# A two-block transformer kernel on one core: retention recast for whole-array matmuls, stick attention's first head readied early, and three smaller edits

## The reference

```python
# experts: out = hb @ w_down, summed with gates; then x = rms_norm(x + y, g_final),
# and the second block begins with h = rms_norm(x, pre_norm_w)
# retention, 4 heads, key width 64, value width 128, chunks of C = 128 tokens
q = rotary(q); k = rotary(k) * (dk ** -0.5)
scores = einsum('bhnid,bhnjd->bhnij', qc, kc) * decay
o_intra = einsum('bhnij,bhnje->bhnie', scores, vc)
chunk_kv = einsum('bhnjd,hj,bhnje->nbhde', kc, k_decay, vc)
state = state * g_chunk + kv                       # over the 8 chunks
o_inter = einsum('bhnid,hi,nbhde->bhnie', qc, q_decay, r_prev)
# stick-breaking attention, 8 heads of width 64
z = einsum('bthd,bshd->bhts', q, k) * scale        # then sigmoids, a reversed
                                                   # running product, and w @ v
# hgrn2, 4 heads: products of q and k with exp of differences of b = cumsum(log_f)
```

## Time and profile before

| what | us |
|---|---|
| median of 3 runs (lowest, highest) | 2588.99 (2585.32, 2596.64) |
| the profiled execution, its own time | 2613.81 |
| its span, first to last instruction | 2612.0 |
| busy: TensorE, VectorE, ScalarE, GpSimd | 2218.1, 1290.0, 1029.8, 584.1 |
| experts' last output copy to first product of `pe` | 1235.96 to 1290.39 |
| retention, first to last TensorE work | 1628.97 to 1699.43 |
| stick attention, first TensorE work | 1715.47 |
| HGRN2, first TensorE work | 2354.51 |

### The profile page before, as it was taken

How to read it: one execution, slowest core, us unless ns; L and a number is a source line. 1 busy time by engine, 2 the same in 40 slices (tenths; PEclk the granted TensorE clock), 3 DMA queues, 4 the chain that set the end, 5 groups by cost and what they waited for, 6 DMA issues and landing times. The chain is left out here.

```text
span 2612.0 us, 34392 instructions
## 1 busy us (share of the span) xinstructions
PE 2218.1 (85%) x12244; PEld 1825.9 (70%) x12244; DVE 1290.0 (49%) x2211; ACT 1029.8 (39%) x1828; POOL 584.1 (22%) x672
## 2 busy tenths in 40 slices
PE   7996997999797599999289997968859799956768
PEld 5885887999685466675278885758748687845657
DVE  3333665555543666665451210357755343417843
ACT  3333654555431255554231210046543233327632
POOL 1003101522010122231110001446522000027822
PEclk9997998999898699999699998579989899987879
DMA  4787776321344399995652312243163424141152
GB/s 152 215 239 198 221 219 165 98 64 40 118 146 171 126 359 370 355 342 209 217 206 97 113 49 77 61 87 73 37 219 108 153 95 148 69 135 47 42 184 90
DMA packets 216721, 399.15 MB, mean 153 GB/s; under 512 B 90513, under 2 KB 111377, under 8 KB 203905
## 3 DMA queue, kind: packets, MB, share of 16 engines
q1 hardware_dynamic: 177008, 314.52, 38.0%
q10 hardware_dynamic: 28384, 61.62, 6.2%
q0 software_dynamic: 11184, 21.13, 2.2%
HBM read 300.16 MB, written 114.85 MB: 159 GB/s over the span
## 5 line engine op out<-in xcount | busy, mean ns | idle before, releaser
L78 PE MATMUL pe_acc<-pe_w,hT 128*128 128x512 f32 x960 | 222.3, 393 | 0.0
L78 PEld LDWEIGHTS pe_acc<-pe_w,hT 128*128 128x128 f32 x960 | 181.7, 190 | 37.8
L78 PE MATMUL ex_gu<-hT,ex_xT 128*128 128x512 f32 x792 | 194.2, 401 | 0.8 <-DVE hT L2349 0.8
L2349 DVE TENSOR_TENSOR hT<-ex_raw,hT 128x2048 fp32r<-128x2048 f32 x66 | 150.9, 2288 | 87.1 <-ACT hT L2320 87.1
L78 PE MATMUL pg_acc<-hT,pg_w 128*128 128x512 f32 x768 | 180.0, 396 | 8.9 <-DVE pg_w L257 8.9
L78 PEld LDWEIGHTS pg_acc<-hT,pg_w 128*128 128x128 f32 x768 | 145.5, 190 | 42.4 <-DVE pg_w L257 9.3
L78 PEld LDWEIGHTS ex_gu<-hT,ex_xT 128*128 128x128 f32 x792 | 147.4, 189 | 34.5 <-DVE hT L2349 1.2
L2320 ACT ACTIVATE hT<-ex_raw 128x2048 fp32r<-128x2048 f32 x66 | 126.2, 1913 | 41.4 <-PEq L47 23.9
L296 DVE COPY pe_o<-pe_acc 128x512 f32<-128x512 f32 x28 | 19.3, 690 | 206.7 <-PE pe_acc L78 206.7
L1725 PE MATMUL ab_op<-ab_v,ab_pT 128*128 128x64 f32 x1024 | 121.3, 272 | 0.0
L2278 PE MATMUL ex_dn<-ex_wd,ex_hT 128*128 128x512 f32 x264 | 118.7, 592 | 0.8 <-ACT ex_hT L2314 0.8
(11 more groups left out here) (473 smaller groups left out, 4990.9 us busy)
## 6 DMA issues: line engine op xcount, KB each, us to landing
ex_raw<-in_w_gate SPq DMA_DIRECT2D x33, 1024.0 KB, 7.2
ex_raw<-in_w_up SPq DMA_DIRECT2D x33, 1024.0 KB, 11.1
ex_wd<-in_w_down SPq DMA_DIRECT2D x33, 1024.0 KB, 14.2
pe_raw<-in_even_w_in SPq DMA_DIRECT2D x6, 2048.0 KB, 9.1
pg_raw<-in_odd_w_in SPq DMA_DIRECT2D x5, 2048.0 KB, 9.4
scr_q<-pa_o SPq DMA_DIRECT2D x32, 256.0 KB, 3.8
scr_k<-pa_o SPq DMA_DIRECT2D x32, 256.0 KB, 3.8
hT<-scr_k SPq DMA_DIRECT2D x16, 512.0 KB, 6.8
```

The source lines that it names most:

```text
L78: mm = pe.matmul(out, a(p, k), b(q, k), start=(k == 0 and i == 0), stop=(k == n - 1 and i == 2))
L2349: dve.tensor_tensor(split(s, LO)[:, :, g, :], raw[:, s % NW, g, :].rearrange("p (k n) -> p k n", k=8), split(s, HI)[:, :, g, :].bitcast(F3 ...
```

## The change

Five edits.

1. **Retention.** Keys are copied into `kz`, one full 128-row block per head with zeros in the other head's 64 rows, and `state` gets a block per head with such zeros, so that scores and q x state contract over 128 rows. The copies from PSUM move from VectorE to ScalarE (four per tile). GpSimd keeps half of the rotation, VectorE takes the other. The state update is four instructions over 64 partitions in place of two over 128. SP loads the first tile ahead of the constants.
2. **Stick attention's first head** is loaded, rounded (ScalarE, at tiles 3 and 4) and its remainders formed (GpSimd, after its rotations) within the retention, into three blocks of hT. The stick stage starts without these steps.
3. **Norms ahead of a projection.** With expert rows, ScalarE does `z` (`act_z`). The first tile's turn comes right behind the weight split on ScalarE and VectorE, and TensorE starts the first product with the first tile alone, doing the second tile's turn after 6 of its 8 blocks. The gain row `prow` is loaded after the first tile's rows.
4. **The loop `further`** has 7 passes with two bodies under one test in place of 14.
5. **HGRN2.** One subtraction per level over all 512, and the sign goes into two Exps of 256. In the first unit VectorE multiplies the keys (`keys_first`), GpSimd the queries.

```diff
@@ project, TensorE @@
+                def first_steps(k):
+                    pe.wait_ge(lo_ok, k + 1)
+                    if r and k == nk - 2:
+                        r.pe_turn(pe, 1)
...
-                            for t in range(j + 1 if j else 0, min(j + 2, NT)):
+                            for t in range(j + 1 if j else 0, min(j + 2, NT) if j else 1):
                                 r.pe_turn(pe, t)
@@ project, ScalarE @@
-                        at_step(s, (r.act_turn, lx + 2, act), (r.act_x, lx, act), (r.act_y, 0, act))
+                        if s > lx + 2:
+                            at_step(s, (r.act_turn, lx + 2, act))
+                        elif lx and s == 2:
+                            r.act_turn(act, 0)
+                        if lx and s > lx + 1:
+                            at_step(s, (r.act_z, lx + 1, act))
+                        at_step(s, (r.act_x, lx, act), (r.act_y, 0, act))
                         if s == 1:
+                            if lx:
+                                r.act_z(act, 0)
                             gains(act)
                             split_hi(act, 0)
+                            if not lx:
+                                r.act_turn(act, 0)
@@ project, VectorE @@
                             split_lo(dve, 0)
-                        at_step(s, (r.dve_turn, lx + 2, dve), (r.dve_x, lx, dve), (r.dve_y, 0, dve))
+                            r.dve_turn(dve, 0)
+                        if s > lx + 2:
+                            at_step(s, (r.dve_turn, lx + 2, dve))
+                        at_step(s, (r.dve_x, lx, dve), (r.dve_y, 0, dve))
@@ Rows @@
+    def act_z(self, act, t):
+        act.wait_ge(self.rs_ok, t + 1)
+        self.x_done(act, t)
+        if t >= 2:
+            act.wait_ge(self.turned, t - 1)
+        for n, (c0, w) in enumerate(self.groups):
+            act.activation(self.z[:, t % 2, c0:c0 + w], self.xs[:, u, c0:c0 + w], ACT.Copy,
+                           scale=self.rs[:, u, n:n + 1]).then_inc(self.z_ok, 1)
@@ further @@
-            with eng.Fori(1, NOV) as j:
-                with eng.If(n > j):
-                    body(j)
+            with eng.Fori(0, (NOV - 1) // 2) as r:
+                with eng.If(n > r * 2 + 1):
+                    for i in range(2):
+                        body(r * 2 + (i + 1))
@@ retention @@
+            def rotate(eng, t, products, step, op, c0, a, b):
+                eng.wait_ge(x_in[t % 4], 16 * (t // 4 + 1))
...
+                eng.tensor_tensor(a[:, u, :, :], first[0], first[1], ALU.mult).then_inc(products, 1)
+                eng.tensor_tensor(b[:, u, :, :], second[0], second[1], ALU.mult).then_inc(products, 1)
+                eng.wait_ge(products, 2 * (t + 1))
+                eng.tensor_tensor(rot[:, t % 4, :, c0:c0 + 32], a[:, u, :, :], b[:, u, :, :], op).then_inc(step, 1)
...
-                            mm = pe.matmul(o, qkT[p0:p0 + 64, u, 4 + j, :], state[p0:p0 + 64, u, j, :], start=False, stop=True)
+                            mm = pe.matmul(o, qkT[:, u, 2 + j, :], state[:, u, h, :], start=False, stop=True)
...
-                            mm = pe.matmul(sps[h % 2][:, j * P:(j + 1) * P], qkT[p0:p0 + 64, u, 2 + j, :], qkT[p0:p0 + 64, u, j, :],
-                                           start=True, stop=True)
+                            mm = pe.matmul(sps[h % 2][:, j * P:(j + 1) * P], kz[:, u, h, :], qkT[:, u, j, :], start=True, stop=True)
...
+                def turn_back(s):
...
+                    act.activation(qkT[:, u, 0:2, :].rearrange("p j n -> p (j n)"), tp[0][:, 0:2 * P], ACT.Copy).then_inc(T_ok, 1)
+                    for b in range(2):
+                        r = slice(64 * b, 64 * b + 64)
+                        act.activation(kz[r, u, :, :].rearrange("p (j b) n -> p j b n", b=2)[:, :, b, :],
+                                       tp[0][r, 2 * P:4 * P].rearrange("p (j n) -> p j n", j=2), ACT.Copy).then_inc(T_ok, 1)
+                    act.activation(qkT[:, u, 2:4, :].rearrange("p j n -> p (j n)"), tp[1][:, 0:2 * P], ACT.Copy).then_inc(T_ok, 1)
@@ stick_breaking, SP @@
-                load_raw(0, 0)
                 sp.dma_start(masks[:, :, :], C["strict"]).then_inc(consts_in, 16)
+                sp.sem_inc(raw_in[0], 64)
+                sp.sem_inc(hi_ok, 8)
+                sp.sem_inc(lo_ok, 8)
@@ hgrn2 @@
-                        act.activation(ex[:, g % 2, :], df[:, g % 2, :], ACT.Exp).then_inc(ex_ok, 1)
+                        for half, sign in enumerate((-1.0, 1.0)):
+                            act.activation(ev[:, :, half, :], dv[:, :, half, :], ACT.Exp, scale=sign).then_inc(ex_ok, 1)
...
-                        dve.tensor_tensor(dv[:, :, 0, :], mid, bv[:, :, 0, :], ALU.subtract).then_inc(df_ok, 1)
-                        dve.tensor_tensor(dv[:, :, 1, :], bv[:, :, 1, :], mid, ALU.subtract).then_inc(df_ok, 1)
+                        dve.tensor_tensor(whole(df[:, g % 2, :], m), whole(b[:, :], m), mid, ALU.subtract).then_inc(df_ok, 1)
+                        if n == 0 and l:
+                            keys_first(l - 1)
```

176 lines of the change are left out of this document (112 added, 64 removed).

## The result

The changed kernel takes 2572.15 us (median of 4 executions, 2562.74 to 2575.03) beside 2590.68 us for the kernel before (4 executions, 2585.32 to 2596.64): a ratio of 0.992, 95% interval 0.9891 to 0.9949. It is faster by 18.5 us, where 47 were forecast; 2572.15 lies above the range of 2532 to 2564. Two later comparisons of the same two kernels gave 0.988 (0.9852 to 0.9907) and 0.9917 (0.9887 to 0.9948). All 19 executions of the changed kernel have a median of 2571.8 us, the 92 of the kernel before in the later comparisons 2591.7: 20 us.

The account below looks back on a forecast made before the run. TensorE was taken as the bound, slowed in the retention by half clock and drains. Terms -29 - 8 - 7 + 0.5 + 0 - 3.5 = -47 us took the median from 2588.99 to 2542, range 2532 to 2564.

Parts of the forecast that it names:

- Gain 29: Whole retention with its earlier start: ends about 1670 in place of 1699.43 us; gain 12 if never at full clock.
- Which clock: Retention: without drains the array works 95% of a step, not 70%, so full clock comes after two steps.
- Retention, one step: Padding removes tiling-mode drains: step 7.6 us for 9.17 at half clock; at full clock TensorE 4.0, step taken as 4.8.
- Retention, whole stage: Retention from first transposes to last output: 45 us, with first scores after 5, one step at 7.6, six at 4.8.
- Retention, start: First tile's rows load first and VectorE shares the rotation: TensorE starts at 1624.5 for 1628.97, gain 4.5 us.
- Stick attention's start: Seam after the retention: first head's loads, roundings and remainders leave the path, masks come first; gain 8 us.
- The loop: Behind the experts: 14 passes at 1.0 us each become seven, 7 us less; nothing if cost follows code jumped over.
- Start of `pe`: Projection behind the experts: first rows 1.7 us sooner, later xs 2.2 us later; net +0.5 us, ends -2 and +3.
- First projection: TensorE begins 1.6 us sooner and waits as long later: 0, ends -1 and +1 us.
- HGRN2: First unit 2.7 us less, later levels 2 less at best, ScalarE 1 more: -3.5 us, ends -6 and +2.
- The rivals: Other outcomes: clock stays half 2559 us (0.25), seams only 2566.5 (0.09), edits not as said 2583 (0.05), slower 2602 (0.01).
- Only the seams gain: Rival, chance 0.09: retention step stays at 9.17 us, set by something else; 22.5 us remain, giving 2566.5.

Follow-up runs that it names:

- before_again: The kernel before, unchanged, run and profiled once more: median 2594.3 us over 12 executions, ratio 1.0003 to the kernel before.
- ret_only: The kernel before with the changed retention alone, stick attention's lead work done in it for nothing: 2584.4 us, ratio 0.9971 to the kernel before.
- ret_old: The changed kernel with the old retention, stick attention's first head still readied inside it: 2580.3 us, ratio 0.9925 to the kernel before.
- after_again: The changed kernel, unchanged, run and profiled once more: 2566.6 us, ratio 0.988 to the kernel before.
- norms_old: The changed kernel with the old order of projections and norms (gain row first, z on VectorE, second transpose group before first product): 2570.1 us, ratio 0.9902 to before.
- after_third: The changed kernel, unchanged, run and profiled a third time: 2572.3 us, ratio 0.9917 to the kernel before.
- before_warm: The kernel before with 36 extra identity matmuls on TensorE ahead of the retention's first transposes: 2591.5 us, ratio 1.0004 to the kernel before.
- pad_only: The kernel before with only the zero-padded keys and state, copied by VectorE, rotation left on GpSimd: 2586.1 us, ratio 0.9962 to the kernel before.
- turn_late: The changed kernel with VectorE's half of the retention's rotation moved behind the state update and mask: 2567.3 us, ratio 0.9906 to the kernel before.

## Why the prediction was wrong

The step that failed is the last one of the sum: "The profiled execution took 2613.81; it would take 2567. The median of before is 2588.99; it would be 2542." It carried 47 us, worked out in an execution 25 us above the median, to the median as if they were the change's own. The term that it was wrong for is the retention's "Gain 29". The runs showed in its place that of the 28.7 us between that execution and before_again's 24.1 stood in the retention: 70.8 us there, 46.7 and 47.1 us in the executions at 2585. Put in alone the changed retention gained 7.0 us at the median (ret_only), taken out it cost 8.5 to 13.7 (ret_old). Against before_again the profiled execution of the changed kernel gains 22.5 us of span: 5.4 behind the experts, 5.0 and 1.6 at the start and in the body of the retention, 9.7 at stick attention's start, and 0.8 net elsewhere.

The profile held what was needed. The earlier trace rows had the output at full clock, 0.212 us a record; with half of the other terms of the earlier trace rows a step of before at full clock comes to 16 x 0.212 + 1.26 + 0.65 = 5.3 us. 5.17 was measured. Against the forecast's own 4.8 us that is a gain of some 3 us over the stage, in place of 24.5, and a sum of 26 us: 2563. The profiled time, 17 us above the slowest of the timed ones, beside the clock of 0.50, was the sign to make that second sum.

By steps:

- *Which clock.* Right for the profiled execution: 1.00 from the third step. The reason, that the old step kept the array at work for only 70% of it, doesn't stand: in before_again the same work ran at 1.00 from the second step on. Nor was 1.00 settled for good, since in two of three executions of the changed kernel it fell again, to windows of 0.66 to 0.71, once VectorE left TensorE idle.
- *Retention, one step.* The drains were right: 0.11 us a record for 0.212, and TensorE alone needs the 4.12 us that the unhindered steps show, for 4.0. (Two readings were off without consequence: the earlier trace rows give 0.45 us a record and 0.11 for 128 columns, not 0.43 and 0.107, and the output's pairs in the step of the earlier trace rows start 0.72 us apart, 0.36 a record and not 0.325.) The size of the step was not right: 5.10 on average for 4.8, and 5.99 in after_again. Two waits that I named stood in it together, where I had taken a value between them: the rotation in line behind its load (4.6 us a step), and the contention of VectorE and GpSimd (5.3, which is 0.4 us for each of four instructions, although show 0.55 for one). Each collision costs what is left of GpSimd's instruction, 0.5 us beside its rotation and 2 us beside the remainders. Those remainders I had called covered, as GpSimd has nothing else to do then. On GpSimd they were; on VectorE they were not.
- *Retention, whole stage.* 45.1 us for 45, which is luck in part: the first scores came 3.66 us behind the first transposes for 5, the first step took 6.57 for 7.6, the next six 30.6 for 28.8, the end 4.3 for 3.6.
- *Retention, start.* -4.2 for -4.5; the first transposes came 7.7 us behind the stage's first transfer, for 7.5.
- *Stick attention's start.* -9.8 for -8: the masks landed in 2.0 us, under the 4.2 that I took from a tile's rows.
- *The loop.* 0.58 us a pass for 1.0: -4.05 for -7. The landing and the barrier, for which I took 4.5 of the 18.52 us, make up 10.4.
- *Start of `pe`.* The first rows came 1.8 us sooner behind GpSimd's first instruction (6.5 us for 8.3), as forecast. Net, up to the end of `pe`, it is +1.1 if the loop's whole 4.05 us count, +2.7 by norms_old, for +0.5; inside its ends.
- *First projection.* No difference that the executions show.
- *HGRN2.* -1.9 and +1.7 in the profiled pair, for -3.5. The first unit gained. The later units lost it, since the step there is GpSimd waiting for the exponentials, and these wait for VectorE's differences. On that chain the edit gives and takes: by the timelines the differences of a level take 0.69 us for 0.76, the exponentials 0.72 for 0.63, so they came no sooner. That this is the whole of the loss is argued, not shown. Lines of before_again and of after, windows of 100 us in the stage (busy us, mean ns, idle us before and its releaser):

```profile
L3020 POOL TENSOR_TENSOR hg_qk<-hg_k,hg_ex 128x256 f32<-128x256 f32 x42 | 32.0, 763 | 19.4 <-ACT hg_ex L2969 19.4
L2969 ACT ACTIVATE hg_ex<-hg_df 128x512 f32<-128x512 f32 x40 | 24.5, 628 | 17.8 <-DVE hg_df L3068 15.1 <-POOL hg_qk L3020 2.3
```
```profile
L3114 POOL TENSOR_TENSOR hg_qk<-hg_k,hg_ex 128x256 f32<-128x256 f32 x42 | 32.2, 766 | 20.6 <-ACT hg_ex L3061 20.5
L3061 ACT ACTIVATE hg_ex<-hg_df 128x256 f32<-128x256 f32 x80 | 28.2, 415 | 15.9 <-DVE hg_df L3167 13.9 <-issue 1.8
```

The direction stood, and so did the three seams, the loop's at little over half its size. The rivals didn't cover the case: each was reckoned from the same execution at 2613.81 us. Nearest in number came "Only the seams gain" (2566.5, given 0.09), and against before_again the retention's body did gain only 1.6 us; but not because the step stayed at 9.17: the old one took 5.17 at full clock.

Still open: why the retention of before runs at half clock for one step or for seven, and where the 7 us between an execution of before at 2585 and its median lie. The retention is not the only stretch that varies: over the twenty profiled executions the one up to the experts' last matmul takes 1232.0 to 1246.8 us (1246.8 in after_third, the slowest of its nine executions) and stick attention 175.8 to 180.8, before and changed alike.

## What to carry to other kernels

Put the profiled execution beside the timed ones before a sum is made; where it lies far from their median, find the stage that differs (a clock at its lower level over a long stretch is the first suspect) and price the change for both levels. When a bound is lifted, the next one may be a queue: here a 4.1 us step was there to be had, but only when a waiting instruction no longer stood ahead of the one that TensorE needed. Work "hidden" on an idle GpSimd is not free while VectorE runs instructions with two inputs in SBUF; give it a stretch where VectorE works from PSUM.

## What the hardware showed that I had not expected

- A VectorE instruction of 0.42 us with two inputs in SBUF took 2.4 to 2.6 us beside a GpSimd instruction of 2.4 to 2.6 us, and 0.82 to 0.95 us beside those of GpSimd's rotation; those with an input in PSUM were untouched.
- The same old retention took 46.7, 47.1, 58.4, 58.8 and 70.8 us in five executions, by how long the granted clock stayed at 0.50, with TensorE's windows full from the second step on (but for the start of before_warm). With every matmul over 128 rows the clock had reached 1.00 by the second scores in all fifteen profiled executions, and the executions lie closer: 12 of pad_only within 10 us, 12 of ret_only within 18, 12 of before_again within 25.
- A clock that had reached 1.00 was lost again in before_warm and in turn_late, behind windows in which TensorE was busy for 2.50 to 3.10 of 5.00 us; in before_warm it then stayed at 0.50 for some 30 us although the windows were full again, in turn_late for 7 and in after_again, twice, for 3.4. Yet the changed kernel's window of 2.81 (1635 to 1640, above) was followed by no fall.
